# Tile 1's GLA output split around tile 0's first head, first experts from an 8 by 8 grid, gather buffers in another order

## The chip, the cores and the metric

One Trainium2 chip, one core of it. The metric is the device time of one execution of the whole program in microseconds (us), the median of several runs. TensorE (PE) multiplies, VectorE (DVE), ScalarE (ACT) and GpSimd (POOL) compute and issue DMAs, SyncE (SP) issues DMAs only, and 16 DMA engines carry the data.

## The reference

Two transformer-like blocks over 256 tokens of width 1024. The first block (recurrent unit, sparse attention, feed-forward) is not touched. The second has two layers, and each is a mixer with a layer norm and then a PEER layer with a layer norm. Layer 0's mixer is gated linear attention (GLA) beside attention over a memory:

```python
o = _gla(q, k, v, log_a)                       # 4 heads, chunks of 64 tokens
o = o * lax.rsqrt(jnp.mean(jnp.square(o), axis=-1, keepdims=True) + HEAD_NORM_EPS)
mix = silu(r) * (o * a_norm_g)
y = concatenate([mix, mo], axis=-1) @ w_out[l]
x = _layer_norm(DN_ALPHA * x + y, ln_mix_g[l], ln_mix_b[l])

q = (xt @ w_q).reshape(T, PEER_HEADS, 2, PEER_HALF)        # PEER: 8 heads
s = einsum('thpe,pne->thpn', q, sub_keys)                  # 2 x 128 key scores per head
top_s, top_i = lax.top_k(s, 16)
cand = top_s[:, :, 0, :, None] + top_s[:, :, 1, None, :]   # 16 x 16 candidates
best_s, best_j = lax.top_k(cand, 16)                       # 16 experts per head and token
expert = top_i[:,:,0][best_j // 16] * 128 + top_i[:,:,1][best_j % 16]
h = einsum('td,thkd->thk', xb, u[eb]); a = gelu(h) * softmax(best_s)
out = einsum('thk,thkd->td', a, v[eb])
```

So per layer every token takes 8 x 16 = 128 experts of 16384, each with a row u and a row v of 1024 floats.

## The kernel before, in words

Tokens lie on the 128 partitions, so the 256 tokens are two tiles, t = 0 and 1. The PEER work is a stream of 512 slots (2 layers x 2 tiles x 128 experts). For slot n GpSimd issues one indirect gather (`L2226`): for each of the 128 tokens of the tile one expert's u and v, 8 KB, into one of 8 buffers (`gbuf`, `GBUF`). VectorE takes the dot product of u with x (`L2510`), ScalarE applies gelu (`L2063`) and scales a diagonal matrix by it and the gate (`L2057`, `L2070`), TensorE multiplies the diagonal with v and adds in a PSUM bank (`add_slot`, `L1444`). That add frees the buffer, and GpSimd may issue gather n + 8.

Everything else of these layers is placed at slot numbers in tables (`pe_steps`, `act_steps`, `dve_steps`): an engine does a slot's steps and then the slot's own work. At slot 1 VectorE adds the mixer's output to tile 1's x (`second_sum`), at 3 it does its layer norm (`second_norm`), for which ScalarE takes the root in slot 2 (`second_root`), at 4 TensorE turns it, and at slots 6 and 9 it does tile 1's part of the first two heads (`tile_head`). From slot 8 on it does the next heads' queries (`head`) for both tiles, with weights from a ring of 8 slots (`weight_ring`), which SyncE fills in pairs, in order, as soon as TensorE has given both slots of a pair back.

The changed place is what stands ahead of slot 0, written out in order for each engine. TensorE: GLA output of tile 0, its mix turned, tile 0's output product (`out_rows`), tile 1's GLA output (`gla_out`, one call per pair of heads and half tile), tile 0's normed x turned (`turn_peer_half`), tile 0's first head (`head_tile`, queries, then `head_tile_keys`, scores), tile 1's mix turned (`turn_mix(1)`), tile 1's output product, tile 0's second head, and only then slot 0. VectorE: `mixed_tile(0)`, the sum and layer norm of tile 0, `mixed_tile(1)`, and then `first_head`, which routes the first head of tile 0: the best key pair (semaphore `first_expert`, gather 0), the next seven (`next_experts`, gathers 1 to 7), the other eight (`peer_experts`). ScalarE takes the squares of each GLA output (`gla_squares`) and copies banks to SBUF (`L1685`).

The gather buffers lie in the arena where the GLA's data lay: buffer place 0 over its queries, place 4 over the mixer's turned output (`mixT`), places 5 to 7 over its values, gates and states; the score rows `sc` overlap the end of the states. So gather 4 waits for tile 1's output (`MIX_BUF`). A wait on a PSUM job is a wait on one counter that TensorE raises per job (`psum_filled`), so jobs are numbered in TensorE's order (`plan`).

## Time and profile before

| what | value |
| --- | --- |
| time, median of 3 runs | 2069.57 us (2065.82 to 2070.25) |
| profiled execution, span | 2068.3 us; the page shows no time around it |
| busy: PE, DVE, ACT, POOL | 92%, 67%, 43%, 29% |
| DMA | 710.15 MB, mean 343 GB/s |
| of it gathers and other software DMAs (q0) | 550.15 MB |
| weights (q1) | 158.34 MB |
| add of slots, L1444 PE, x2048 | 975.7 us busy |
| dot of slots, L2510 DVE, x512 | 618.3 us busy, 448.3 idle before, of it 444.8 for the gather |

The page cuts the span into 40 slices and gives the busy share of each engine and of the DMA engines; windows do the same for any stretch. A timeline lists an engine's groups of instructions in order, with the idle time ahead of a group and what ended it. A 128x512 fp32 product leaves two records in the profile, so an add of a slot (two products) leaves four. Gather n is the n-th row of L2226.

### The profile page before, as it was taken

The page shows a single profiled execution, that of the slowest core. Times are in us where ns is not written, and L with a number is a line of the kernel's source. Part 1 is how long each engine was busy: PE and PEld are TensorE (multiplying, and loading weights), DVE is VectorE, ACT ScalarE, POOL GpSimd, SP SyncE. Part 2 cuts the span into 40 slices and gives each one's busy share as a digit, 9 for nine tenths or more (in the row PEclk, how much of TensorE's full clock was granted, in tenths as well). Part 3 has the DMA queues.
Part 4 walks back from the last instruction along what each step waited for, and adds up shares of the span by engine and source line. Part 5 has one row for each costly group of instructions (what it writes and reads, how often), then busy time and mean ns, then how long its engine had stood idle before and what let it go on. Part 6 is the DMA issues. An engine that isn't in the chain of part 4 may idle for free. (4 is left out here: it accounts for less than half of the span.)

```text
span 2068.3 us, 24678 instructions
## 1 busy us (share of the span) xinstructions
PE 1893.4 (92%) x8012; PEld 1183.8 (57%) x8012; DVE 1384.0 (67%) x2957; ACT 896.7 (43%) x2417; POOL 609.3 (29%) x563
## 2 busy tenths in 40 slices
PE   8999999999998999987999998889999989778776
PEld 7888678887964655533565534546675455332222
DVE  7788566666738776899534645667856466994444
ACT  5657454444634343344324623333455334343332
POOL 0002200000003434444433344333334433444442
PEclk9999999999999999999999999999999999999999
DMA  6633555554649999999999999999999999999997
GB/s 241 223 135 109 204 194 183 189 177 164 221 156 367 411 421 410 421 414 410 421 421 421 421 421 421 421 421 398 421 421 402 418 422 420 421 419 421 421 422 308
DMA packets 99373, 710.15 MB, mean 343 GB/s; under 512 B 11041, under 2 KB 11185, under 8 KB 14385
## 3 DMA queue, kind: packets, MB, share of 16 engines
q0 software_dynamic: 76928, 550.15, 64.6%
q1 hardware_dynamic: 22176, 158.34, 20.2%
q8 instruction: 64, 1.05, 0.2%
q14 instruction: 61, 0.49, 0.1%
q10 hardware_dynamic: 144, 0.11, 0.0%
HBM read 707.51 MB, written 1.05 MB: 343 GB/s over the span
## 5 line engine op out<-in xcount | busy, mean ns | idle before, releaser
L1444 PE MATMUL bank<-arena 128*128 128x512 f32 x2048 | 975.7, 614 | 147.9 <-ACT arena L2070 146.7
L2510 DVE SCALAR_TENSOR_TENSOR arena<-arena,x_tok 128x1024 f32<-128x1024 f32 x512 | 618.3, 1225 | 448.3 <-DMA arena<-peer_uv,arena 444.8
L2226 POOL DMA_INDIRECT arena<-peer_uv,arena x512 | 576.4, 1126 | 876.4 <-PE bank L1444 630.7
L1444 PEld LDWEIGHTS bank<-arena 128*128 128x128 f32 x2048 | 374.6, 194 | 629.7 <-issue 341.5
L2063 ACT ACTIVATE arena<-arena 128x1 f32<-128x1 f32 x512 | 103.1, 201 | 831.7 <-DVE arena L2510 830.8
L913 PEld LDWEIGHTS bank<-xT,weight_ring 128*128 128x128 f32 x1376 | 184.3, 194 | 39.1 <-issue 31.5
L2057 ACT ACTIVATE arena<-const_tile,arena 128x128 f32<-128x128 f32 x512 | 198.3, 387 | 0.0
L2070 ACT ACTIVATE arena<-arena 128x128 f32<-128x128 f32 x512 | 197.8, 386 | 0.8
L913 PE MATMUL bank<-xT,weight_ring 128*128 128x128 f32 (+1 forms) x1376 | 194.4, 295 | 0.8 <-DVE xT L2253 0.8
L913 PE MATMUL bank<-x_low_high,z_high 128*128 128x512 f32 (+1 forms) x480 | 135.5, 350 | 0.0
L1189 PE MATMUL bank<-x_split,w_split 128*128 128x512 f32 x704 | 129.2, 342 | 2.8 <-DVE x_split L2790 2.8
L1189 PEld LDWEIGHTS bank<-x_split,w_split 128*128 128x128 f32 x704 | 110.5, 191 | 20.2 <-issue 3.0
L2772 DVE TENSOR_TENSOR w_split<-weight_ring,w_split 128x1024 fp32r<-128x1024 f32 x66 | 80.8, 1225 | 36.8 <-ACT w_split L1898 36.0
L913 PE MATMUL bank<-x_low_high,ring_low 128*128 128x256 f32 x368 | 104.1, 283 | 0.0
L913 PEld LDWEIGHTS bank<-x_low_high,z_high 128*128 128x128 f32 x480 | 83.8, 191 | 14.9 <-issue 2.9
L1685 ACT ACTIVATE arena<-bank 128x512 f32<-128x512 f32 (+6 forms) x143 | 67.9, 499 | 53.0 <-PE bank L913 52.2
L859 POOL DMA_DIRECT2D row_ring<-rows_in x8 | 4.5, 571 | 288.1 <-DVEq L2326 200.8
L1898 ACT ACTIVATE w_split<-weight_ring 128x1024 fp32r<-128x1024 f32 x66 | 69.8, 1061 | 42.4 <-PE bank L1189 26.6
L913 PE MATMUL bank<-arena 128*64 128x128 f32 (+10 forms) x664 | 72.6, 305 | 1.7 <-DVE arena L2276 1.0
L913 PEld LDWEIGHTS bank<-x_low_high,ring_low 128*128 128x128 f32 x368 | 70.3, 191 | 0.0
L913 PEld LDWEIGHTS bank<-arena 64*128 64x128 f32 (+6 forms) x664 | 52.2, 161 | 26.6 <-issue 22.8
L913 PE MATMUL bank<-weight_ring,arena 128*128 128x512 f32 (+1 forms) x192 | 64.9, 528 | 0.2 <-ACT arena L1685 0.2
(321 smaller groups left out, 1991.9 us busy)
## 6 DMA issues: line engine op xcount, KB each, us to landing
weight_ring<-weights SPq DMA_DIRECT2D x149, 1024.0 KB, 4.9
arena<-peer_uv,arena POOLq DMA_INDIRECT x512, 13.7
row_ring<-rows_in POOLq DMA_DIRECT2D x8, 512.0 KB, 4.9
arena<-weights POOLq DMA_DIRECT2D x5, 512.0 KB, 7.9
kept_keys<-weights POOLq DMA_DIRECT2D x4, 512.0 KB, 10.0
const_tile<-consts POOLq DMA_DIRECT2D x1, 1657.0 KB, 8.3
x_tok<-x_in SPq DMA_DIRECT2D x2, 512.0 KB, 4.6
memT<-memT_in POOLq DMA_DIRECT2D x1, 1024.0 KB, 8.4
```

The lines of the kernel that those rows point to most:

```text
L859: e.dma_start(rows[:, n % NROW, :], rows_in[n:n + 1, :].to_broadcast([P, D]))\
L913: ins = pe.matmul(o, lhsT, rhs, start=start, stop=stop, is_transpose=turn or None)
L1189: ins = pe.matmul(o, lhsT, rhs, start=start, stop=stop)
L1444: ins = pe.matmul(b[:, :], diag[n % DIAGS], gbuf[n % GBUF][:, 1, h * 512:(h + 1) * 512], start=n % P == 0, stop=n % P == P - 1)
L1685: done(act.activation(o, i, f, **kw), "drained_by_act" if last else "act_step")
L1898: done(act.activation(w_split[n % SPLITS][:, 0, :], ring[:, slot % RING, :], ACT.Copy), "slot_high")
L2057: done(act.activation(gate_diag[n % 2], ident, ACT.Copy, scale=w[:, s:s + 1]), "gate_diag")
L2063: done(act.activation(hdot[:, s:s + 1], hdot[:, s:s + 1], ACT.Gelu), "peer_gelu")
L2070: done(act.activation(diag[n % DIAGS], gate_diag[n % 2], ACT.Copy, scale=hdot[:, s:s + 1]), "diag_ready")
L2226: pool.indirect_dma_start(gbuf[n % GBUF].rearrange("p a d -> p (a d)"), None, peer_uv, bass.IndirectOffsetOnAxis(ap=expert[t][:, s:s + 1]. ...
L2510: dve.scalar_tensor_tensor(u, u, 1.0, x[:, t, :], ALU.mult, ALU.mult, accum_out=hdot[:, s:s + 1])\
L2772: done(dve.tensor_tensor(w[:, 1, :], ring[:, slot % RING, :], w[:, 0, :], ALU.subtract), name)
```

## The change

Four edits. (1) TensorE: all but a part of tile 1's GLA output stands directly behind tile 0's output product; the second half tile of its last two heads stands around the scores of tile 0's first head. Of tile 1's output product, the three remaining pieces of its first two rows move behind that head, and the ring slots of these rows are given back there. (2) VectorE: the first expert and the next seven are found ahead of `mixed_tile(1)`, the latter from a grid of 8 by 8 candidates and not 16 by 16; the other eight come behind it, from a 16 by 16 grid into whose corner the 8 by 8 grid is copied with its best eight struck out. (3) ScalarE's order follows. (4) `GATHER_PLACES` gives gathers 0 to 7 the places 0, 1, 2, 3, 5, 6, 7, 4; gather 0 waits also for the last GLA product, gather 5 for tile 1's mix, gather 7 for tile 1's output.

TensorE, from tile 0's output product to slot 0, before (64x192: GLA output; x_tok: turn of x; xT,arena: head; weight_ring: output product; L1444: slots):

```order
L913 MATMUL bank<-weight_ring,arena 128x512 x16
L913 MATMUL bank<-arena 64x192 x4
L913 MATMUL bank<-const_tile,x_tok 128x128 x4
L913 MATMUL bank<-arena 64x192 x4
L913 MATMUL bank<-const_tile,x_tok 128x128 x4
L913 MATMUL bank<-arena 64x192 x8
L913 MATMUL bank<-xT,arena 128x128 x16
L913 MATMUL bank<-const_tile,arena 128x128 x8
L913 MATMUL bank<-weight_ring,arena 128x512 x12
L913 MATMUL bank<-xT,arena 128x128 x16
L913 MATMUL bank<-const_tile,arena 128x128 x2
L1444 MATMUL bank<-arena 128x512 x8
```

and the same place now:

```order
L914 MATMUL bank<-weight_ring,arena 128x512 x13
L914 MATMUL bank<-arena 64x192 x12
L914 MATMUL bank<-const_tile,x_tok 128x128 x8
L914 MATMUL bank<-xT,arena 128x128 x16
L914 MATMUL bank<-arena 64x192 x2
L914 MATMUL bank<-const_tile,arena 128x128 x2
L914 MATMUL bank<-arena 64x192 x2
L914 MATMUL bank<-weight_ring,arena 128x512 x3
L914 MATMUL bank<-const_tile,arena 128x128 x6
L914 MATMUL bank<-weight_ring,arena 128x512 x12
L914 MATMUL bank<-xT,arena 128x128 x16
L914 MATMUL bank<-const_tile,arena 128x128 x2
```

Three of the sixteen output products have moved from ahead of the first turn of x to ahead of the mix's turn (the row of x6), and of the sixteen GLA products all but four stand ahead of the turns. The x8 of const_tile,arena before is the mix's turn (6) and the keys (2), in this order.

VectorE, behind tile 0's layer norm, before (128x4 and 128x192: tile 1's mix; the rest: routing of the first head):

```order
L2941 RECIPROCAL arena<-arena 128x4
L2945 SCALAR_TENSOR_TENSOR arena<-bank,arena 128x192 x4
L2438 MAX arena<-arena 128x8 x2
L2441 MAX_INDEX arena<-arena 128x8 x2
L2443 CAST arena<-arena 128x2x8
L2444 TENSOR_SCALAR arena<-arena 128x1
L2445 TENSOR_TENSOR arena<-arena 128x1
L2448 MATCH_REPLACE arena<-arena 128x128 x2
```

and now, from the last three instructions of the next experts on:

```order
L2431 TENSOR_REDUCE arena<-arena 128x7
L2433 TENSOR_SCALAR arena<-arena 128x7
L2434 TENSOR_TENSOR arena<-arena 128x7
L2960 RECIPROCAL arena<-arena 128x4
L2964 SCALAR_TENSOR_TENSOR arena<-bank,arena 128x192 x4
L2471 MATCH_REPLACE arena<-arena 128x128 x2
L2474 MAX arena<-arena 128x8 x2
```

Tile 1's mix stood ahead of all routing, and stands now behind the experts 0 to 7. Between the first expert and the mix there are 16 instructions (lines 2456 to 2434).

The diff, cut:

```diff
@@ -40,7 +40,7 @@
 EXPERTS = PN * PN
 ALPHA = 4.0 ** 0.25
 GBUF = 8
-MIX_BUF = 4
+GATHER_PLACES = (0, 1, 2, 3, 5, 6, 7, 4)
 DIAGS = 5
 CARRY = 24
 LATER = 3
@@ -381,13 +381,13 @@
     plan("gla_o", 2, "dve", [0, 1])
     plan("gla_mixT_0", 2, "act", [6, 7])
     plan("out0_0", 2, "dve", [2, 3])
+    plan("gla_o", 1, "dve", [0], first=2)
     plan("xT_peer0_0", 1, "act", [6])
-    plan("gla_o", 1, "dve", [0], first=2)
     plan("xT_peer0_0", 1, "act", [7], first=1)
...
@@ -782,11 +782,12 @@
         mem_E = [area(24016 + 512 * b, 2, S) for b in range(3)]
         mem_PT = [area(25552 + 512 * b, 4, P) for b in range(2)]
 
-        gbuf = [area(2 * D * b, 2, D) for b in range(GBUF)]
         lo = 2 * D * GBUF
+        gbuf = [area(2 * D * b, 2, D) for b in GATHER_PLACES]
         sc = [area(lo + 2048 * t, 16, PN) for t in range(NT)]
         pq = [area(lo + 4096 + 512 * b, 2, S) for b in range(2)]
         rest = area(lo + 5120, 2 * TH * PN)
+        first_grid = area(lo + 5120 + 2 * PN, PK * PK // 4)
         onehot = area(lo + 5120, TH, PK, PK)
         top_v, top_i, top_f = (area(lo + 5632 + 64 * n, 2 * TH, PK) for n in range(3))
         best_v, best_j, pos_a, pos_b, sel_a, sel_b, pos_u = (area(lo + 5824 + 32 * n, TH, PK) for n in range(7))
@@ -1280,14 +1281,14 @@
                             mm(b[0:GDK, i * GDV:(i + 1) * GDV], kendT[o, n // 2, h, :],
                                gv[o, n // 2, h * GDV:(h + 1) * GDV], True, True, end=i == 1)
 
-                def gla_out(t, hp, pars):
+                def gla_out(t, hp, pars, heads=range(2)):
 
                     key = ("gla_o", 2 * t + hp)
                     b = begin(key) if pars[0] == 0 else bank(key)
                     for par in pars:
                         n = 2 * t + par
                         o = slice(par * CH, (par + 1) * CH)
-                        for i in range(2):
+                        for i in heads:
                             h = 2 * hp + i
                             vcol = slice(h * GDV, (h + 1) * GDV)
                             last = par == 1 and i == 1
@@ -1393,22 +1394,23 @@
             for h in range(2):
                 for k in range(NK - 2):
                     out_rows(0, k, [h])
-            out_rows(1, NK - 2, [1])
-            out_rows(1, NK - 1)
-            give_back()
-            gla_out(1, 0, [0])
+            gla_out(1, 0, range(2))
+            gla_out(1, 1, [0])
             pe.wait_ge(sem("x_half_ready"), 1)
             turn_peer_half(0, 0)
-            gla_out(1, 0, [1])
             pe.wait_ge(sem("x_ready"), 5)
             turn_peer_half(0, 1)
-            gla_out(1, 1, range(2))
             wait_drained(pe, ("xT_peer0_0", 1))
             pe.wait_ge(sem("head_loaded"), 64)
             head_tile(0, 0, 0)
             head_tile(0, 1, 0)
+            gla_out(1, 1, [1], [0])
+            head_tile_keys(0, 0)
+            gla_out(1, 1, [1], [1])
+            out_rows(1, NK - 2, [1])
+            out_rows(1, NK - 1)
+            give_back()
             turn_mix(1)
-            head_tile_keys(0, 0)
             wait_drained(pe, ("gla_mixT_1", 1))
             for k in range(NK - 2):
                 out_rows(1, k)
@@ -2077,13 +2079,13 @@
                 gla_squares(i)
             mix_turned(0)
             norm_root(0, 0)
+            gla_squares(2)
             turned_peer_half(0, 0)
-            gla_squares(2)
             turned_peer_half(0, 1)
+            head_tile(0, 0)
+            head_tile_keys(0, 0)
             gla_squares(3)
-            head_tile(0, 0)
             mix_turned(1)
-            head_tile_keys(0, 0)
             gate_exp(0, 0, 0, 1)
             head_tile(1, 0)
             head_tile_keys(1, 0)
@@ -2211,6 +2213,7 @@
             for n in range(SLOTS):
                 l, t, s = slot_of(n)
                 if n == 0:
+                    wait_filled(pool, ("gla_o", 3))
                     pool.wait_ge(sem("first_expert"), 1)
                 elif n == 1:
                     pool.wait_ge(sem("next_experts"), 1)
@@ -2218,7 +2221,9 @@
                     pool.wait_ge(sem("peer_experts"), ROUTE_NO[0, 0, 0])
                 elif (l, t, s) in ROUTE_NO:
                     pool.wait_ge(sem("peer_experts"), ROUTE_NO[l, t, s])
-                if n == MIX_BUF:
+                if n == GATHER_PLACES.index(6):
+                    pool.wait_ge(sem("mix_ready"), 2)
+                if n == GATHER_PLACES.index(4):
                     wait_filled(pool, ("out0_1", 1))
                 if n >= GBUF:
                     wait_freed(pool, n - GBUF)
@@ -2411,29 +2416,28 @@
...
-            def ranks_to_experts(l, t, h, first, last, name):
+            def ranks_to_experts(first, last, bits, name):
...
-            def first_head():
+            def first_expert():
+
+                half = PK // 2
                 wait_drained(dve, ("peer_s0_0_0", 0))
...
@@ -2444,6 +2448,25 @@
                 step(dve.tensor_scalar(sel_a[:, 0, 0:1], top_f[:, 0, 0:1], float(PN), 0.0, ALU.mult, ALU.add))
                 step(dve.tensor_tensor(expert[0][:, 0:1].bitcast(U32), sel_a[:, 0, 0:1], top_f[:, 1, 0:1], ALU.add),
                      "first_expert")
+
+            def next_experts():
+
+                half, lowest = PK // 2, -3.0e38
+                grid = rest[:, 0:half * half]
+                step(dve.tensor_tensor(grid.rearrange("p (a b) -> p a b", a=half),
+                                       top_v[:, 0, 0:half].unsqueeze(2).to_broadcast([P, half, half]),
+                                       top_v[:, 1, 0:half].unsqueeze(1).to_broadcast([P, half, half]), ALU.add))
+                best, at = best_v[:, 0, 0:half], best_j[:, 0, 0:half].bitcast(U32)
+                step(dve.max(best, grid))
+                step(dve.max_index(at, best, grid))
+                step(dve.match_replace(first_grid, best, grid, lowest))
+                ranks_to_experts(1, half, 3, "next_experts")
+
+            def other_experts():
+
+                half, lowest = PK // 2, -3.0e38
+                keys = sc[0][:, 0:2, :]
+                left = rest[:, 0:2 * PN].rearrange("p (a n) -> p a n", a=2)
                 for q in range(2):
                     done(dve.match_replace(left[:, q, :], top_v[:, q, 0:half], keys[:, q, :], lowest), "dve_step")
                 settle()
@@ -2455,20 +2478,16 @@
                 settle()
                 step(dve.tensor_copy(top_f[:, 0:2, half:PK], top_i[:, 0:2, half:PK].bitcast(U32)))
                 flat = keys.rearrange("p a n -> p (a n)")
-                step(dve.tensor_tensor(flat.rearrange("p (a b) -> p a b", a=PK),
-                                       top_v[:, 0, :].unsqueeze(2).to_broadcast([P, PK, PK]),
+                grid = flat.rearrange("p (a b) -> p a b", a=PK)
+                step(dve.tensor_tensor(grid, top_v[:, 0, :].unsqueeze(2).to_broadcast([P, PK, PK]),
                                        top_v[:, 1, :].unsqueeze(1).to_broadcast([P, PK, PK]), ALU.add))
+                step(dve.tensor_copy(grid[:, 0:half, 0:half], first_grid.rearrange("p (a b) -> p a b", a=half)))
                 best, at = best_v[:, 0, :], best_j[:, 0, :].bitcast(U32)
-                step(dve.max(best[:, 0:half], flat))
-                step(dve.max_index(at[:, 0:half], best[:, 0:half], flat))
-                ranks_to_experts(0, 0, 0, 1, half, "next_experts")
-                others = rest[:, 0:2 * PN]
-                step(dve.match_replace(others, best[:, 0:half], flat, lowest))
-                step(dve.max(best[:, half:PK], others))
-                step(dve.max_index(at[:, half:PK], best[:, half:PK], others))
+                step(dve.max(best[:, half:PK], flat))
+                step(dve.max_index(at[:, half:PK], best[:, half:PK], flat))
                 step(dve.tensor_tensor(gate_w[0][:, 0, :], best, best[:, 0:1].to_broadcast([P, PK]), ALU.subtract),
                      "peer_shifted")
-                ranks_to_experts(0, 0, 0, half, PK, "peer_experts")
+                ranks_to_experts(half, PK, 4, "peer_experts")
                 normalised_gates(0, 0, 0, 1)
 
             def experts(l, t, h, size):
@@ -2974,8 +2993,10 @@
             mixed_tile(0)
             first_sum()
             first_norm()
+            first_expert()
+            next_experts()
             mixed_tile(1)
-            first_head()
+            other_experts()
             for n in range(SLOTS + 2 * LATER + 1):
                 for name, what in DVE_STEPS.get(n, []):
                     if name == "second_sum":
```

## Rows read from the trace of the kernel before

**Rows 1.** The page's second part: DMA busy tenths in 40 equal slices.
```profile
DMA  6633555554649999999999999999999999999997
```

**Rows 2.** Windows around tile 1's mix: busy per engine, PEclk, DMA share, GB/s.
```profile
610.00:615.00 5.00, 5.00 (x24) 2.12 (x22) 0.00 (x0) 1.45 (x6) 0.00 (x0) 1.00 0.34 143
615.00:620.00 5.00, 5.00 (x42) 4.63 (x42) 1.57 (x5) 1.71 (x7) 0.00 (x0) 1.00 0.00 0
624.00:628.00 4.00, 4.00 (x11) 1.75 (x10) 3.65 (x15) 0.00 (x0) 1.00 (x1) 1.00 0.57 176
628.00:632.00 4.00, 4.00 (x16) 2.19 (x15) 3.55 (x15) 0.22 (x1) 1.23 (x2) 1.00 1.01 406
640.00:644.00 4.00, 3.87 (x6) 1.26 (x5) 2.10 (x3) 1.90 (x4) 0.48 (x1) 0.50 1.01 426
```

**Rows 3.** TensorE timeline: start, us, line, out<-in, count [idle before <- releaser].
```profile
606.85 1.94 PE L913 MATMUL bank<-arena 64*64 64x192 f32 x8
...
615.50 3.84 PE L913 MATMUL bank<-xT,arena 128*128 128x128 f32 x32
619.18 1.35 PE L913 MATMUL bank<-const_tile,arena 128*128 128x128 f32 x10
620.74 10.57 PE L913 MATMUL bank<-weight_ring,arena 128*128 128x512 f32 x24 [0.21 <-ACT arena L1685]
631.14 3.73 PE L913 MATMUL bank<-xT,arena 128*128 128x128 f32 x32
635.35 0.71 PE L913 MATMUL bank<-const_tile,arena 128*128 128x128 f32 x4 [0.47 <-ACT arena L1685]
...
638.92 6.56 PE L1444 MATMUL bank<-arena 128*128 128x512 f32 x8 [2.86 <-ACT arena L2070]
```

**Rows 4.** VectorE timeline, same columns, 617 to 648 us.
```profile
617.19 1.39 DVE L2945 SCALAR_TENSOR_TENSOR arena<-bank,arena 128x192 f32<-128x192 f32 x4
620.99 0.49 DVE L2438 MAX8 arena<-arena 128x8 f32<-128x128 f32 x2 [2.42 <-ACT arena L1685]
...
626.90 0.28 DVE L2423 TENSOR_TENSOR arena<-const_tile,arena 128x112 f32<-128x112 f32 x1
...
629.36 0.17 DVE L2429 TENSOR_TENSOR arena<-arena 128x7 uint32<-128x7 f32 x1
...
636.34 1.28 DVE L2519 SCALAR_TENSOR_TENSOR x_tok<-x_tok,bank 128x512 f32<-128x512 f32 x2
...
640.73 1.23 DVE L2510 SCALAR_TENSOR_TENSOR arena<-arena,x_tok 128x1024 f32<-128x1024 f32 x1 [1.56 <-DMA arena<-peer_uv,arena]
...
644.60 0.16 DVE L2340 RECIPROCAL arena<-arena 128x1 f32<-128x1 f32 x1 [0.24 <-ACT arena L1693]
...
647.77 1.23 DVE L2510 SCALAR_TENSOR_TENSOR arena<-arena,x_tok 128x1024 f32<-128x1024 f32 x1 [0.15 <-DVE x_tok L2343]
```

**Rows 5.** GpSimd timeline, same columns: gathers 0, 1 and 18.
```profile
623.99 1.01 POOL L2226 DMA_INDIRECT arena<-peer_uv,arena  x1 [32.53 <-issue]
630.47 0.98 POOL L2226 DMA_INDIRECT arena<-peer_uv,arena  x1 [5.46 <-DVE arena L2429]
...
677.58 0.94 POOL L2226 DMA_INDIRECT arena<-peer_uv,arena  x1 [3.46 <-PE bank L1444]
```

**Rows 6.** DMA issues, median us to landing: windows 623:625, 638:640, 677:679.
```profile
arena<-peer_uv,arena POOLq DMA_INDIRECT x1, 5.6
...
arena<-peer_uv,arena POOLq DMA_INDIRECT x2, 16.8
...
arena<-peer_uv,arena POOLq DMA_INDIRECT x1, 6.3
```

**Rows 7.** Windows, columns as in Rows 2, beside the first heads.
```profile
660.00:670.00 10.00, 10.00 (x41) 6.63 (x40) 8.16 (x24) 5.46 (x13) 1.92 (x2) 1.00 1.01 421
...
680.00:684.00 4.00, 4.00 (x20) 2.85 (x19) 2.11 (x12) 0.66 (x2) 1.27 (x3) 1.00 0.95 354
```

**Rows 8.** TensorE timeline: tile 1's first head at slot 6.
```profile
657.09 3.73 PE L913 MATMUL bank<-xT,arena 128*128 128x128 f32 x32
```

More of the change, by code:

```diff
@@ L2412, in best_pairs @@
                                        ALU.subtract), "peer_shifted")
-            def ranks_to_experts(l, t, h, first, last, name):
-                n = last - first
-                oh = onehot[:, 0, 0:n]
+            def ranks_to_experts(first, last, bits, name):
+                n, side = last - first, 1 << bits
+                oh = onehot[:, 0, 0:n, 0:side]
                 for q, (pos, sel) in enumerate(((pos_a, sel_a), (pos_b, sel_b))):
-                    op, val = (ALU.logical_shift_right, 4) if q == 0 else (ALU.bitwise_and, 15)
+                    op, val = (ALU.logical_shift_right, bits) if q == 0 else (ALU.bitwise_and, side - 1)
                     pos, sel, at = pos[:, 0, 0:n], sel[:, 0, 0:n], pos_u[:, 0, 0:n].bitcast(U32)
```

16 lines of the change are left out of this document (7 added, 9 removed).

## The prediction

> **What bounds the kernel now.** I read the page's slices of the DMA engines first [rows 1]. From the thirteenth slice (some 620 us) to the thirty-ninth they are nine tenths busy or more: the stream of 512 expert gathers and the weight loads fill them, and rows 7 give that stream's rate, 421 GB/s. Before it the load is light. So the kernel has two parts: a front whose length is set by the engines, and a stream whose length is set by bytes. The change works on the seam, so I went there. Windows [rows 2] show the seam: 0.34 busy in 610 to 615 (one pair of weight slots, 1.05 MB, is loaded there), nothing in 615 to 620, 0.57 in 624 to 628 with the lone first gather, then full. The timelines of TensorE, VectorE and GpSimd [rows 3 to 5] give the chain: scores of tile 0's first head at 620.99, first gather issued at 623.99, the next at 630.47.
>
> The next question is whether the stream is bound by bytes from its first microsecond on. It is not. A gather issued at about 639 lands 16.8 us later, one issued alone 5.6 us later, and gather 18, issued at 677.58, lands 6.3 us later [rows 5, 6]: the queue had nearly run dry, and in 680 to 684 the DMA share falls to 0.95 and the rate to 354 GB/s [rows 7]. Gather 18 waits for its buffer, and its releaser is the weighted add on TensorE (L1444). TensorE is busy for 10.00 of 10 us in 660 to 670 [rows 7], where it has the heads' queries to do between the adds. So between the start of the stream and slot 18 TensorE's chain eats the lead of the DMA queue, and at slot 18 it is TensorE's chain, not the first gather, that says when the stream goes on. Every microsecond by which that chain is later is a microsecond of the end; a gather that starts earlier buys nothing if the lead is used up anyway.
>
> **The change part by part, first gather.** The three output products (0.44 us a record [rows 3], two records each) leave the path: the GLA output follows at 606.85 - 3 x 0.88 = 604.2. It issues 24 records before the turns, at 1.94 / 8 = 0.24 each: 610.0. Eight turning products, at 1.35 / 10 each, give 611.1, and the copy of the second half about 0.9 more: head at 612.0 instead of 615.50 [rows 3]. After 3.68 of head come four GLA records (0.9), in which ScalarE copies the queries out, then the keys, 0.5: done at 617.1. Before, TensorE's row of turns and keys ends at 620.53 and VectorE starts at 620.99, so now 617.6, 3.4 us earlier, and the first gather is issued at about 620.6 instead of 623.99. Its new wait, for the last GLA product, ends at about 618 and hides behind that. GpSimd has nothing else queued there.
>
> **Second gather.** From gather 0 to gather 1 before: 630.47 - 623.99 = 6.5 us [rows 5]. Now 16 listed VectorE instructions lie between, the smallest like the 0.17 of L2429, the widest under the 0.28 of 112 elements [rows 4], with some 0.03 between them: 3.2 to 5.0 us, I take 3.8. Gather 1 is issued at 624.4, 6.1 us earlier. Gathers 2 to 4 follow freely; gather 5 waits for tile 1's mix (625.0, hidden), gather 7 for tile 1's output.
>
> **What the same reordering costs.** VectorE ran tile 1's mix at 617.19 for 1.39 us, with a reciprocal ahead, before the scores came [rows 4]: it was free there, since VectorE stood idle for 2.42 us behind it. Now it comes behind the next experts: 617.6 + 1.9 + 3.8 = 623.3, and 1.6 us for it gives 625.0. TensorE has by then done the last GLA records (to 618.0) and the three output products (to 620.7) and waits 4.4 us. Behind that wait are queued, in order, the turn of the mix, tile 1's output, the second head and the add of slot 0. The turn starts at 625.1 instead of 619.18, and from its start to the output it takes 1.56 as before [rows 3]: output at 626.7 instead of 620.74, **6.0 us later**. Output (10.4), head (3.7) and keys last as before, so the output is done at 637.2 and the add of slot 0 starts at 638.92 + 6.0 = 644.9.
>
> Not all of this reaches slot 18, for there was slack: before, VectorE's dot of slot 1 waited 1.56 us for its gather [rows 4]. It ended at 641.96 and the reciprocal of tile 1's layer norm came 2.64 later, at 644.60; between lie slot 1's work on ScalarE, a table load and the root. Now the gather is there long before, and ScalarE can do slot 1 only after slot 0, so the root follows the add of slot 0: 644.9 + 2.6 = 647.5, 2.9 us later than 644.60. The sum into tile 1 (636.34 before) starts at 637.2 and does not decide. From the reciprocal on the order is as it was: dot of slot 3 at 647.77 + 2.9, the head at slot 6 at 657.09 + 2.9 [rows 4, 8], and TensorE without a gap from there to slot 10, which frees gather 18's buffer.
>
> **The clock.** TensorE's gap of 2.86 us at 636 [rows 3] was followed by a granted clock of 0.50 in 640 to 644 [rows 2], that is 1.2 GHz and not 2.4, and the eight records behind it took 6.56 us where 8 x 0.44 = 3.5 is normal. So such a gap has cost 3.0 us. The new gap of 4.4 us stands ahead of the turn and the output; the old one stays. Its price is between 0 and 3.0; part of the slow time falls into the gap itself and into the wait for the mix's copy, and I take 1.2, of which half shows at slot 3 since VectorE and ScalarE have little slack there: 0.6. The Trainium skill (TensorE: Matmul & The Clock Gate, "The HAM clock gate") says that the half clock is the state of an idle array and that activity releases it; by that rule the new gap costs its full slow time, 1.2 us or more on the sum, and the trace agrees with the mechanism, with its 0.50.
>
> **What comes back.** Before, the stream already lost (421 - 354) x 4 / 421 = 0.6 us in 680 to 684 [rows 7] while gather 17 was still running; now the queue is dry ahead of 18 and the two no longer share. Between 0 and 1.1 us returns; I take 0.5.
>
> **The sum.** 2.9 + 0.6 - 0.5 = +3.0 us, bounds 2.9 - 1.1 = 1.8 and 2.9 + 3.0 = 5.9. The profiled span is 2068.3 us and nothing is shown around it: 2071.3. It lies 1.3 under the median of 2069.57, so the median should be **2072.6**. Reordering the buffers, the smaller grid and the 64-element copy cost some 0.3 us of VectorE ahead of slot 0, hidden behind tile 1's output (experts ready at about 632, output at 637.2).
>
> **Rivals.** (a) *Slower by more.* The chain from the late mix is worse than summed: both gaps give slow adds, gather 8 is issued only after slot 0's slow add (about 650 to 652), slots 3 to 6 are spread out, and the dry queue lasts longer. It decides from the point where slot 6's head starts later than about 661.5. At 6.0 us the whole delay of slot 0 reaches the end: 2068.3 + 6 = 2074.3, the median 2075.6. For it: rows 7 show no idle TensorE time to catch up with. Against it: the 1.56 us of slack in rows 4. (b) *Bytes bind.* If the stream's start counts and not slot 18, the lead of 3.4 us is kept. But the weight pair that lay in idle time at 610 to 612 is freed only by the first turn of the mix, now at 625, in full traffic: 1.05 MB / 421 GB/s = 2.5 us. Net -0.9, or up to -1.7 with the 0.8 us lost between gathers 0 and 1. Median 2068.3. For it: rows 1. Against it: the 6.3 us of gather 18 [rows 6]. The Trainium skill (DMA: Bandwidth & Descriptors, "Where 436 GB/s comes from") has a load from HBM bound at some 358 GB/s; by that the pair would cost 2.9 us and the net be -0.5, but the trace has 421 and decides. (c) *A real gain.* Gather 1's 6.1 us count, and the pair is absorbed: up to -5, median 2064.6. It needs a dry stream at its start and a full one at slot 18, and rows 2 show it full from 628 on.
>
> **How the numbers follow.** Forecast 50%, (a) 24%, (b) 20%, (c) 6%. A change under 0.2% (4.1 us) can't be told from none here. The forecast (1.8 to 5.9 with the medians' own scatter of some 2 us) is slower by over 0.2% in a quarter of its cases, (a) in five sixths, (b) hardly, (c) faster in most: faster 0.06, same 0.61, slower 0.33. The range leaves out (c) and the worst of (a): 2066.5 to 2077.0; the forecast's own is 2070 to 2075.5.
>
> **What would show it.** First gather issued near 620.6 and second near 624.4; the mix of tile 1 near 623.5; a TensorE gap of over 4 us near 621 to 625 with a clock of 0.5 behind it; tile 1's output from about 626.7; slot 0's add at 645 to 646; slot 6's head at 660 to 661.5; a DMA share under 1 before gather 18's data at about 681 to 684. The prediction is wrong if slot 6's head does not start later than 657, or if it does and the DMA engines are never idle before 690.

## The result: what the change did to the time

| | before | changed |
|---|---|---|
| median of 6 runs, us | 2069.74 (2065.82 to 2071.30) | 2074.82 (2073.99 to 2076.96) |
| span of the profiled execution, us | 2068.3 | 2072.8 |
| granted clock of TensorE, mean | 0.983 | 0.983 |

The ratio of the times is 1.0029, 95% interval 1.0019 to 1.0039: the changed kernel is slower, by 5.1 us by the medians and 6.0 by the ratio. The span of its profiled execution is 4.5 us longer, so the two profiles show the effect. Its own time is 2074.57 us, 1.8 over its span. One slow execution of the kernel before, of 10812.59 us, which fell among the later runs, is left out of all ratios below.

The page's DMA slices have the shape of [rows 1]: light up to the twelfth slice (three of the first twelve read a tenth lower), full from the thirteenth on:

```profile
DMA  6633555544539999999999999999999999999997
```

Everything ahead of the seam is in step. VectorE aggregates the statistics of tile 0's layer norm at 605.91 us before and at 605.95 now; I count from this point (**the anchor**) wherever kernels are compared below, since the work ahead of it ends some us earlier or later from run to run (at 602.7 to 611.0 in the runs below).

TensorE's timeline of the changed kernel, to be held against [rows 3, 8]:

```profile
604.32 5.68 PE L914 MATMUL bank<-arena 64*64 64x192 f32 x24
...
611.83 3.84 PE L914 MATMUL bank<-xT,arena 128*128 128x128 f32 x32 [0.80 <-ACT xT L1687]
...
616.53 0.71 PE L914 MATMUL bank<-const_tile,arena 128*128 128x128 f32 x4
...
618.11 2.84 PE L914 MATMUL bank<-weight_ring,arena 128*128 128x512 f32 x6
625.19 1.54 PE L914 MATMUL bank<-const_tile,arena 128*128 128x128 f32 x6 [4.24 <-DVEq L2968]
627.26 12.15 PE L914 MATMUL bank<-weight_ring,arena 128*128 128x512 f32 x24 [0.54 <-ACT arena L1687]
639.25 3.73 PE L914 MATMUL bank<-xT,arena 128*128 128x128 f32 x32
643.46 0.71 PE L914 MATMUL bank<-const_tile,arena 128*128 128x128 f32 x4 [0.47 <-ACT arena L1687]
647.03 7.11 PE L1446 MATMUL bank<-arena 128*128 128x512 f32 x12 [2.86 <-ACT arena L2072]
...
661.79 3.73 PE L914 MATMUL bank<-xT,arena 128*128 128x128 f32 x32
```

Tile 0's head starts at 611.83 instead of 615.50. Then comes the gap of 4.24 us, its releaser VectorE's mix, and behind it the turn at 625.19 instead of 619.18. From the turn's start to the next head it now takes 2.1 us more (14.06 us, not 11.96, though the keys' products no longer stand in between). Slot 0's add starts 8.1 us later, slot 6's head 4.70 us later.

VectorE [rows 4]. The 0.17 us row of L2434 is the last of the next experts, the row of L2964 tile 1's mix, now behind them; the reciprocal is that of tile 1's layer norm:

```profile
617.76 0.49 DVE L2442 MAX8 arena<-arena 128x8 f32<-128x128 f32 x2 [7.83 <-ACT arena L1687]
...
623.28 0.17 DVE L2434 TENSOR_TENSOR arena<-arena 128x7 uint32<-128x7 f32 x1
...
623.70 1.39 DVE L2964 SCALAR_TENSOR_TENSOR arena<-bank,arena 128x192 f32<-128x192 f32 x4
...
641.74 1.22 DVE L2529 SCALAR_TENSOR_TENSOR arena<-arena,x_tok 128x1024 f32<-128x1024 f32 x1
...
649.52 0.16 DVE L2345 RECIPROCAL arena<-arena 128x1 f32<-128x1 f32 x1 [5.40 <-ACT arena L1695]
```

The dot of slot 1 at 641.74 waits for no gather any more (1.56 us before), and VectorE then stands 5.40 us ahead of the reciprocal, which comes at 649.52 instead of 644.60.

GpSimd [rows 5], gathers 0, 1, 7, 8 and 18:

```profile
620.74 1.01 POOL L2231 DMA_INDIRECT arena<-peer_uv,arena  x1 [29.23 <-issue]
624.39 0.98 POOL L2231 DMA_INDIRECT arena<-peer_uv,arena  x1 [2.64 <-DVE arena L2434]
...
640.43 0.94 POOL L2231 DMA_INDIRECT arena<-peer_uv,arena  x1 [8.86 <-PE bank L914]
651.14 1.99 POOL L2231 DMA_INDIRECT arena<-peer_uv,arena  x1 [9.78 <-issue]
...
682.28 0.94 POOL L2231 DMA_INDIRECT arena<-peer_uv,arena  x1 [4.23 <-PE bank L1446]
```

Gathers 0 and 1 are issued 3.25 and 6.08 us earlier. Gather 8, which needs the buffer that slot 0's add frees, is 7.6 us later counted from the anchor, and gather 18 is 4.70 us later. Two things come before that. The lead is gone at gather 7, which waits for tile 1's output (place 4) and is issued 1.6 us later than before, behind the anchor, where gather 6 was still 6.9 us earlier. And gather 18 is not alone: from gather 11 to gather 52 every one is issued 4.4 to 4.8 us later, nearly all of them 4.65; TensorE's adds free their buffers. I go on naming gather 18, as the prediction does. The windows [rows 2, 7] show what the stream makes of that:

```profile
624.00:628.00 4.00, 2.27 (x7) 1.64 (x8) 3.66 (x18) 1.64 (x3) 2.85 (x3) 0.50 0.85 289
628.00:632.00 4.00, 4.00 (x8) 1.62 (x7) 3.59 (x14) 0.73 (x2) 2.81 (x3) 0.69 1.00 420
...
652.00:656.00 4.00, 3.56 (x10) 1.30 (x9) 3.81 (x13) 1.57 (x6) 3.15 (x3) 1.00 0.96 369
656.00:660.00 4.00, 3.19 (x15) 1.60 (x13) 3.86 (x13) 1.87 (x5) 0.95 (x2) 1.00 0.97 350
...
670.00:680.00 10.00, 10.00 (x41) 7.17 (x40) 8.03 (x18) 3.03 (x12) 3.48 (x3) 1.00 0.87 301
```

In 624 to 628 the DMA engines are at 0.85 where they were at 0.57: the stream does start earlier. What it gains is lost in hollows, at 652 to 660 (369 and 350 GB/s) and at 670 to 680 (301 GB/s at a share of 0.87, with TensorE busy for the whole 10 us). From 670 to 692 (344 GB/s in the last 12 us) the traffic that is missing against 421 GB/s is (120 x 10 + 77 x 12) / 421 = 5.0 us; before it was 1.3 us by the same sum (411 and 384 GB/s). The clock of 0.50 and 0.69 in the first two rows is the one behind the new gap.

### The profile page after: what moved, and what is told of

It is laid out like the page before. It is cut to its first block and busy times, and to the rows that moved or that the text cites. A ratio compares the mean times of both kernels' runs of the same rounds, so it can differ in the third digit from the quotient of the medians.

```text
span 2072.8 us, 24681 instructions
## 1 busy us (share of the span) xinstructions
PE 1892.0 (91%) x8012; PEld 1183.8 (57%) x8012; DVE 1383.4 (67%) x2959; ACT 896.3 (43%) x2417; POOL 611.7 (30%) x563
```

## The experiments

**Theory A**, that of the prediction: tile 1's mix is late, so TensorE's chain from the turn to slot 18 is late, and that chain sets when the stream goes on; early gathers buy nothing. **Theory B**, its rival: the bytes bind from the start of the stream, and a pair of weight slots that was loaded in idle time is now loaded in full traffic. (It is: the load of 1024 KB issued in 605 to 612 landed after 4.9 us before, and the one issued in 624 to 630 takes 10.1 us now.) All ratios are to the kernel before, timed on the same chip; a ratio need not equal the quotient of the two medians. Times in the last four columns are us behind the anchor.

| kernel | median, us | ratio (95%) | gather 0 | slot 0's add | gather 18 | end of span |
|---|---|---|---|---|---|---|
| before | 2069.74 | | 18.08 | 33.01 | 71.67 | 1462.39 |
| changed | 2074.82 | 1.0029 (1.0019 to 1.0039) | 14.79 | 41.08 | 76.33 | 1466.85 |
| changed, again | 2076.69 | 1.0045 (1.0032 to 1.0058) | 14.79 | 41.88 | 77.12 | 1468.98 |
| mix between | 2067.05 | 0.9992 (0.9982 to 1.0001) | 14.80 | 35.14 | 70.38 | 1460.64 |
| mix first | 2069.13 | 0.9996 (0.9987 to 1.0005) | 18.35 | 35.13 | 71.10 | 1462.05 |
| mix later still | 2081.76 | 1.0063 (1.0048 to 1.0078) | 14.79 | 49.04 | 84.28 | 1474.12 |
| pair early | 2078.32 | 1.0035 (1.0021 to 1.0050) | 17.36 | 45.03 | 80.28 | 1471.68 |
| grid only | 2068.33 | 0.9999 (0.9990 to 1.0008) | 18.08 | 33.01 | 70.45 | 1460.77 |
| clock kept up | 2073.81 | 1.0021 (1.0010 to 1.0031) | 14.79 | 39.05 | 74.30 | 1466.58 |
| light, changed | 2072.30 | 1.0011 (0.9999 to 1.0023) | 14.78 | 41.86 | 71.93 | 1464.71 |
| light, before | 2069.86 | 0.9998 (0.9988 to 1.0009) | 18.09 | 33.02 | 68.77 | 1462.66 |
| table early, before | 2069.42 | 1.0004 (0.9995 to 1.0012) | 18.09 | 33.89 | 71.37 | 1462.09 |
| mix between, table early | 2068.88 | 0.9994 (0.9984 to 1.0005) | 14.80 | 33.42 | 71.47 | 1462.12 |

The kernel before had medians of 2069.08 to 2069.74 in the four groups of runs.

### Tile 1's mix directly behind the first expert

```diff
             first_expert()
-            next_experts()
             mixed_tile(1)
+            next_experts()
             other_experts()
```

> The changed kernel with one move: VectorE does tile 1's mix between the first expert and the next seven. Theory A (the late mix delays TensorE's chain, and that chain at slot 18 sets the end): the mix ends at about 621.2 instead of 625.1, TensorE's gap of 4.2 us shrinks to some 0.4, its clock does not fall there, slot 0's add starts at about 641 instead of 647.0 and slot 6's head at about 656 to 657 instead of 661.8. The time comes back to that of the kernel before or 1 us below it: 2068.5 to 2070, 5 us under the changed kernel. Theory B (bytes bind; the weight pair that lost its idle slot is the cost): gather 1 is issued 1.7 us later than in the changed kernel and the pair 3.9 us earlier, still in traffic; under 1 us of change, about 2074.

TensorE's timeline, which starts 2.7 us earlier here (the anchor is at 603.26), and the window that was hollow, taken at the same place behind the anchor:

```profile
618.60 0.87 PE L914 MATMUL bank<-const_tile,arena 128*128 128x128 f32 x6 [0.34 <-DVEq L2968]
620.22 10.57 PE L914 MATMUL bank<-weight_ring,arena 128*128 128x512 f32 x24 [0.74 <-ACT arena L1687]
...
638.40 7.11 PE L1446 MATMUL bank<-arena 128*128 128x512 f32 x12 [2.86 <-ACT arena L2072]
...
653.16 3.73 PE L914 MATMUL bank<-xT,arena 128*128 128x128 f32 x32
```

```profile
667.00:677.00 10.00, 10.00 (x39) 6.40 (x38) 4.91 (x10) 4.62 (x17) 4.64 (x4) 1.00 1.00 395
```

The gap is down to 0.34 us, the turn and the output take their old 0.87 and 10.57 us, slot 6's head is 5.9 us earlier than in the changed kernel behind the anchor, the window has a DMA share of 1.00 and 395 GB/s, and the whole loss is gone (2067.05, under both forecasts). Gather 0 is where it was and gather 1 is 1.7 us later than in the changed kernel. One line of VectorE's order carries the loss; the earlier GLA output, the smaller grid and the buffers' order all stay in. The pair comes earlier too: its load is issued 15.8 us behind the anchor and lands after 7.0 us, for the most part beside gather 0 alone, where it was 19.9 and 10.1. That could give back B's 2.5 us at most, and 6.2 came back at the end of the span. Theory A.

### Tile 1's mix ahead of the first expert, as before

```diff
             first_norm()
+            mixed_tile(1)
             first_expert()
             next_experts()
-            mixed_tile(1)
```

> The changed kernel with VectorE's old order: tile 1's mix ahead of all routing. TensorE, ScalarE and the buffer places stay as changed. The mix must wait for the late GLA products: it ends at about 621.1, the first gather is issued at about 624.1 (as before the change) and the next at about 627.9, 3.4 us later than in the changed kernel. Theory A: slot 0's add at about 641, slot 6's head at 656 to 657, the time that of the kernel before, 2069 to 2070. Theory B: the stream starts 3.4 us later than in the changed kernel, with the weight pair still in traffic: 2076 to 2078.

Gather 0 is now at 18.35, 3.6 us later than in the changed kernel, and gather 1 at 22.01, 3.6 later too. The end is 4.8 us earlier all the same, and the median, 2069.13, is where A put it; B had 2076 to 2078. The pair is not still in traffic, as I had expected: its load is issued 15.8 us behind the anchor, ahead of gather 0, and lands after 4.7 us. With 2.5 us back for that and a start 3.6 us later, B still has the end 1 us later. A later start of the stream with an end that much earlier is what B can't have.

### The mix later still

```diff
                 ranks_to_experts(half, PK, 4, "peer_experts")
+                mixed_tile(1)
                 normalised_gates(0, 0, 0, 1)
...
             next_experts()
-            mixed_tile(1)
             other_experts()
```

> The changed kernel with the same wait made longer: tile 1's mix stands behind the routing of all 16 experts of the first head, only the gates' norm comes after it. Theory A: the mix ends 7.3 us later (about 632.3), TensorE's gap grows to about 11.5 us, slot 0 and slot 6's head come 7 us later, and so does the end: 2082. Theory B: the gathers are issued as before but for 5 and 6, and the bytes are the same: 2075 to 2076.

```profile
629.40 1.54 PE L914 MATMUL bank<-const_tile,arena 128*128 128x128 f32 x6 [11.63 <-DVEq L2969]
631.48 12.72 PE L914 MATMUL bank<-weight_ring,arena 128*128 128x512 f32 x24 [0.53 <-ACT arena L1687]
```

The mix is 7.4 us later than in the changed kernel, the gap 7.4 us longer, gather 18 is 8.0 us and the end 7.3 us later, with gathers 0 and 1 where they were. The medians differ by 6.9 us, where B had at most 1. Once the slack is used up, a microsecond of the mix is about one of the end.

### The pair of weight slots freed in idle time

```diff
+            out_rows(1, NK - 2, [1])
+            out_rows(1, NK - 1)
+            give_back()
             gla_out(1, 0, range(2))
...
             gla_out(1, 1, [1], [1])
-            out_rows(1, NK - 2, [1])
-            out_rows(1, NK - 1)
-            give_back()
             turn_mix(1)
```

> The changed kernel with the first three output products of tile 1 and the giving back of their ring slots ahead of the GLA output, as before the change. The weight pair moves in idle time again. Theory A: everything behind is later by the 2.6 us of these products (first gather at about 623.3, the mix ends at about 627.7, TensorE's gap stays, slot 6's head at about 664.4), the time about 2077. Theory B: 2.5 us of bytes leave the busy time and the stream starts 2.6 us later: 2075, no change.

```profile
630.24 1.54 PE L914 MATMUL bank<-const_tile,arena 128*128 128x128 f32 x6 [7.03 <-DVEq L2968]
```

This takes away B's cost: the pair is loaded by 614, in idle time, in 4.8 us. But it also makes the stream start 2.6 us later, so that B had forecast no change (2075) and A 2077. The three products and their pair are back ahead of the head, so head, scores, mix and turn are all 2.6 us later, and the gap grows by the work that was moved out of it. The output then takes 13.53 us and not 12.15, so that gather 18 is 4.0 us and the end 4.8 us later than in the changed kernel. That is more than A needs, but the profiled execution, 2081.91, was the slowest of five. The ratio, 1.0035, lies between the two of the changed kernel. By the times this experiment decides nothing; B fell with the three before it.

### The smaller grid alone, on the kernel before

The kernel before, with `first_expert()`, `next_experts()` and `other_experts()` of the changed kernel in the place of `first_head()`; the mix stays ahead.

> The kernel before with one part of the change: the next seven experts come from the 8 by 8 grid; the orders of all engines, the mix ahead of the routing and the buffer places are those of before. Gather 1 is issued at about 627.9 instead of 630.5. Theory A: slot 0's add stays at 638.9, the dot of slot 1 no longer waits 1.6 us for gather 1, the layer norm of tile 1 and slot 6's head come 1.5 us earlier, and the end 1.1 to 1.5 us earlier: 2068.4. Theory B: the stream starts 2.6 us earlier with the weight pair still in idle time, up to 2.6 us less: 2067.2.

VectorE, the dots of slots 1 and 2 and the reciprocal (the anchor is at 603.03):

```profile
635.81 1.23 DVE L2525 SCALAR_TENSOR_TENSOR arena<-arena,x_tok 128x1024 f32<-128x1024 f32 x1
...
638.42 1.23 DVE L2525 SCALAR_TENSOR_TENSOR arena<-arena,x_tok 128x1024 f32<-128x1024 f32 x1 [1.37 <-DMA arena<-peer_uv,arena]
...
639.69 0.16 DVE L2341 RECIPROCAL arena<-arena 128x1 f32<-128x1 f32 x1
```

Gather 1 is 2.9 us earlier and its dot waits no more; the next dot then waits 1.37 us for gather 2. Of the 2.9 us, 1.2 reach gather 18, and the times resolve no gain (0.9999), though the profile ends 1.6 us earlier. The change's own profit is therefore small even where nothing spoils it.

### Dummy products in the gap

```diff
             give_back()
+            for i in range(4):
+                pe.matmul(ps[2][:, :], ident, c("keysT"), start=True, stop=True)
             turn_mix(1)
```

> The changed kernel with four products of 128x512 (constants, result never read) that TensorE does while it waits for tile 1's mix. Theory A with the clock as a part of it: the wait of 4.2 us is mostly filled, the granted clock stays at 1.00 through the turn and tile 1's output, these take 2.1 us less (0.8 and 10.6 instead of 1.5 and 12.15), slot 6's head starts at about 659.7, and the time falls by 1.5 to 2.1 us to about 2073. If the clock costs nothing at the end, and theory B: no change, 2075.

TensorE, and the window of its turn and output:

```profile
621.05 3.60 PE L1414 MATMUL bank<-const_tile 128*128 128x512 f32 x8
...
625.47 0.87 PE L914 MATMUL bank<-const_tile,arena 128*128 128x128 f32 x6 [0.82 <-DVEq L2970]
627.09 10.57 PE L914 MATMUL bank<-weight_ring,arena 128*128 128x512 f32 x24 [0.74 <-ACT arena L1689]
...
660.03 3.73 PE L914 MATMUL bank<-xT,arena 128*128 128x128 f32 x32
```

```profile
625.00:629.00 4.00, 2.79 (x11) 1.60 (x12) 3.63 (x18) 2.16 (x3) 3.08 (x4) 1.00 0.84 289
```

The four products leave eight records. The turn starts at the same moment as in the changed kernel (625.47 with an anchor 0.27 later), so nothing but the clock differs, 1.00 where it was 0.50: 0.87 us against 1.54, 10.57 against 12.15. Slot 0's add, slot 6's head and gather 18 all come 2.0 us earlier. So in this pair of executions the clock's price is 2.25 us on the two rows and 2.0 on the chain (0.2 goes into the wait for the mix's copy, 0.54 us against 0.74). At the end the profile shows 0.3 us of it, and the ratios (1.0021 against 1.0029 and 1.0045) overlap. Issues of later gathers, us behind the anchor, say where it went:

| gather | 18 | 48 | 64 | 256 | 500 |
|---|---|---|---|---|---|
| before | 71.7 | 150.9 | 196.7 | 736.4 | 1407.9 |
| changed | 76.3 | 155.6 | 200.0 | 741.1 | 1412.4 |
| clock kept up | 74.3 | 153.5 | 200.1 | 739.9 | 1412.1 |
| mix between | 70.4 | 150.1 | 195.5 | 735.2 | 1406.2 |
| mix later still | 84.3 | 163.5 | 209.1 | 748.5 | 1419.8 |
| changed, again | 77.1 | 156.4 | 201.4 | 742.7 | 1414.6 |
| light, changed | 71.9 | 154.5 | 198.6 | 738.2 | 1410.3 |
| light, before | 68.8 | 150.2 | 197.3 | 736.8 | 1408.2 |

The 2.0 us stand at gather 48 and are gone at 64. The stretch from 48 to 64 took 44.1 to 47.1 us in the thirteen traces, so an execution loses or gains 1 to 2 us there whatever went before. The two executions of the changed kernel lie 0.8 us apart at gather 18 and 2.1 at the end. Whether the clock's 2 us reach the end is not settled.

### TensorE relieved

```diff
                 w = next_weights()
-                for k in range(NK):
+                for k in ((0, NK - 1) if h == 2 else range(NK)):
                     mm(b[:, q * S:(q + 1) * S], w[:, k * P:(k + 1) * P], xT[:, k, :], k == 0, k == NK - 1,
```

This edit was made to the changed kernel and to the kernel before. It leaves out six of the eight pieces of each query product of the third head.

> The changed kernel, with most of the queries of the third head left out: six of eight 128-row pieces of each of its two products (slots 8 and 10), so its routing is of another head; all gathers, dots and adds stay. TensorE has 5.4 us less to do ahead of slot 10's add, which frees gather 18's buffer. Theory A: gather 18 is issued up to 5.4 us earlier than at 682.3, the hollow in the DMA rate between 670 and 692 (5 us of traffic missing by the changed kernel's windows) fills, and the time falls by 3 to 5 us, to 2070 to 2072. Theory B: the same bytes, no change, 2075.

> The kernel before with the same queries of the third head left out. Its DMA rate misses only 1.1 us of traffic in 680 to 688. Theory A: about 1.1 us less, 2068.6, so that the two kernels with the light head differ by 1.5 to 3 us instead of 5. Theory B: no change, 2069.7, and the difference stays 5.

```profile
675.00:685.00 10.00, 10.00 (x31) 5.28 (x31) 8.78 (x21) 6.06 (x24) 6.34 (x6) 1.00 0.95 310
685.00:697.00 12.00, 12.00 (x44) 7.49 (x43) 8.61 (x30) 3.33 (x13) 4.88 (x5) 1.00 0.96 399
```

The rows are of the changed kernel so relieved (anchor at 610.99, 5 us later, so they are the stretches 670 to 680 and 680 to 692 of above). Gather 18 comes 4.4 us earlier than in the changed kernel, but the first stretch stays hollow (310 GB/s, 301 above) and only the second fills (399, 344 above): the missing traffic falls from 5.0 us to 3.3. Its median falls from 5.1 us over the kernel before to 2.4 over the relieved kernel before. That one gains nothing by the same edit, though its gather 18 is 2.9 us earlier; I had expected 1.1 us of it.

How the half came back is not shown. Of the 4.4 us at gather 18, 1.0 are left at gather 48, and the two relieved kernels stand 3.2 us apart at gather 18, 4.3 at gather 48 and 1.3 at gather 64: the difference shrinks in the stretch in which executions scatter by 1 to 2 us, not where TensorE was relieved. In both, gather 18 now lands 10.7 us after its issue and gathers 25 to 35 after 12 to 18 (8 to 13 in the kernels with the full head), so the queue is fuller there, and a gather that is issued earlier waits longer. By that reading TensorE's chain paces the stream in the kernels as they are, and relieved of 5.4 us of work no longer does. A holds for the delay and not for a gain of any size.

### The gelu's table loaded ahead of tile 1's head

```diff
             gate_exp(0, 0, 0, 1)
+            gate_diagonal(0)
+            done(act.activation(tmp_sq[:, GDV:GDV + 1], c("eps")[:, 0:1], ACT.Gelu), "act_step")
             head_tile(1, 0)
             head_tile_keys(1, 0)
-            gate_diagonal(0)
```

This takes the table load out of the 2.86 us gap of [rows 3], once on the kernel before and once together with the mix between.

> The kernel before with the same move on ScalarE alone (gate diagonal and gelu table ahead of the copies of the second head). Slot 0's add comes 1.6 us earlier, but the root of tile 1's layer norm waits for the dot of slot 1, which waits for gather 1 until 640.7 as before. Theory A: slot 6's head and gather 18 stay where they were and the time too, 2069.5, within 1 us. If slot 0's add alone set the end: 1.6 us less.

> The kernel of the first experiment (mix between first and next experts) with one more move on ScalarE: slot 0's gate diagonal and the load of the gelu table (by a gelu of one constant) stand ahead of the copies of the second head, no longer between the scores' copy and slot 0. TensorE's gap ahead of slot 0 (2.86 us) falls by 1.28 + 0.3 to about 1.2 us, its clock does not fall behind it, slot 0's add, the layer norm of tile 1 and slot 6's head come some 1.6 us earlier. Theory A: gather 18 is issued 1.6 us earlier; from there bytes bind, so of that at most the 1.4 us come back that the first experiment's windows still miss: 2065.5 to 2067.5, under both kernels. Theory B: nothing in the bytes is changed, as the first experiment.

On the kernel before, the move failed at what it was for: slot 0's add came 0.9 us later (33.89 against 33.01 behind the anchor), not 1.6 earlier. ScalarE's diagonal now waits 3.69 us for the gates from VectorE, ahead of the copies of the second head, and TensorE waits 2.56 us for these ahead of the keys (anchor at 604.71):

```profile
634.00 0.40 ACT L2057 ACTIVATE arena<-const_tile,arena 128x128 f32<-128x128 f32 x1 [3.69 <-DVE arena L2504]
...
636.24 1.22 PE L913 MATMUL bank<-const_tile,arena 128*128 128x128 f32 x4 [2.56 <-ACT arena L1685]
```

Gather 18 and the time stayed, but as slot 0's add was not made earlier, the question that was meant, whether that add alone sets the end, stays untested.

TensorE with both, anchor at 605.88:

```profile
639.30 3.70 PE L1446 MATMUL bank<-arena 128*128 128x512 f32 x8 [1.15 <-ACT arena L2072]
...
653.38 2.76 PE L1446 MATMUL bank<-arena 128*128 128x512 f32 x4 [1.95 <-ACT arena L2072]
655.95 4.65 PE L914 MATMUL bank<-xT,arena 128*128 128x128 f32 x32
```

The gap falls to 1.15 us and the eight records behind it take 3.70 us, not 6.56. Yet slot 6's head starts where it did with the mix between alone (50.07 against 49.90): a gap of 1.95 us appears at slot 5 and the head behind it takes 4.65 us instead of 3.73. Slot 0's add is 1.7 us earlier, as expected, but the saving turned into a later wait: gather 18 is 1.1 us later than with the mix between alone, not 1.6 earlier, and the median, 2068.88, misses the 2065.5 to 2067.5 that I had expected. No kernel of this study is measurably faster than the one before; the nearest is the mix between, at 0.9992 with an interval that reaches 1.0001.

### The changed kernel once more

The changed kernel, with no edit, beside the last two.

> The changed kernel itself, beside the two others on one chip, to have its ratio from the same run of rounds: 1.0029 of the kernel before, within 0.001.

It gave 1.0045 (1.0032 to 1.0058) beside the first 1.0029 (1.0019 to 1.0039), more than the 0.001 off that I had allowed. It is slower both times; what the two intervals share, 1.0032 to 1.0039, is 6.6 to 8.1 us, and their ends are 3.9 and 12 us. The loss is certain and its size is not. TensorE (anchor at 604.72) and the window behind slot 0's gap:

```profile
623.97 1.41 PE L914 MATMUL bank<-const_tile,arena 128*128 128x128 f32 x6 [4.26 <-DVEq L2968]
625.91 13.07 PE L914 MATMUL bank<-weight_ring,arena 128*128 128x512 f32 x24 [0.54 <-ACT arena L1687]
...
646.60 3.70 PE L1446 MATMUL bank<-arena 128*128 128x512 f32 x8 [2.86 <-ACT arena L2072]
```

```profile
647.00:651.00 4.00, 3.30 (x8) 1.14 (x6) 1.84 (x3) 3.86 (x7) 1.61 (x1) 1.00 1.02 424
```

The same gap of 4.26 us here makes the turn and the output 3.04 us longer, not 2.25. And the old gap of 2.86 us, behind which the kernel before had a clock of 0.50 and 6.56 us for eight records, has a clock of 1.00 behind it and 3.70 us. What a gap's slow clock takes is not one number. Nor does it always reach the chain: in seven traces (the changed kernel twice, mix between, mix later still, pair early, clock kept up, light changed) slot 6's head starts 14.76 or 14.77 us behind slot 0's add, with the slow clock behind the old gap or without it.

## Why the prediction held, and which term was too small

The time of 2074.82 us lies in the range (2066.5 to 2077.0), 2.2 over the forecast of 2072.6. The mechanism was right. The size was low by a half or more: +3.0 us forecast, 4.5 between the two profiles, 5.1 between the medians, 6.0 and 9.3 by the two ratios. With it I gave "slower by over 0.2%" too little, 0.33.

- **First and second gather.** Forecast 620.6 and 624.4, measured 620.74 and 624.39. Each was a sum of row durations on VectorE and TensorE, and such sums held to 0.1 us.
- **The late mix and the gap.** Mix done 625.0 forecast, 625.09 measured; gap 4.4 and 4.24; turn 625.1 and 625.19.
- **The clock: the mis-sized term.** I took 1.2 us for it, counted half, 0.6, and had argued that part of the slow time would fall into the gap and the wait for the mix's copy. Only 0.2 does: the turn and the output take 0.67 and 1.58 us more, 2.25 together, of which the dummy products gave 2.0 back as far as gather 18. In the repeat they take 3.04 more. The half for slack at slot 3 was wrong too: the 2.1 us by which slot 0's add was later than forecast (8.1 and not 6.0) were 2.0 at the reciprocal. My own bounds, 0 to 3.0, held it as it reached the chain. The old gap of 2.86 us had shown 3.0, and going by it would have come closer, but partly by luck: behind the same gap the repeat shows nothing, and in the changed order what was slow there never reached slot 6's head. What I had wrong is the place. The new gap stands ahead of the output product, and behind it TensorE works on through the second head with waits of 0.54 and 0.47 us only, so that its own rows are the chain and the slow time has little slack to fall into.
- **The slack.** 2.9 of the 6.0 us were to remain at the reciprocal, 2.6 us behind slot 0's add. Measured 2.49 behind it, and 4.92 us late, that is the 2.9 and 2.0 of clock. Slot 0's add itself came at 647.03, outside my 645 to 646, by the same 2.0.
- **On to slot 18.** "From the reciprocal on the order is as it was" held: +4.70 at slot 6's head and +4.70 at gather 18. That slot 18 is the place where the chain takes over did not: the delay has its 4.7 us from gather 11 on and keeps them to gather 52.
- **What comes back.** 0.5 forecast, 0.2 measured. In all 2.9 + 2.0 - 0.2 - 0.2 = 4.5 us, the difference of the spans (the first 0.2 from the reciprocal to slot 3's dot, the second behind gather 18). That this closes is a matter of these two executions: the delay is 3.2 us at gather 64 and 4.7 at 256, and the profile of the repeat stands 5.5 us behind at gather 18 and 6.6 at the end. The 0.5 is neither confirmed nor refuted.
- **Rival (a)** was to decide from 661.5 at slot 6's head; 661.79 is just past it. Its mark, gather 8 at 650 to 652, came true with 651.14, but not its price: of slot 0's 8.1 us 4.7 reached the end, since the 1.56 us wait and what lay behind it did absorb the rest. The case lies between the forecast and (a).
- **Rival (b)** fell with the mix put first, between and later still. Granted the pair's 2.5 us wherever its load had moved out of the traffic, it has the end 1 us later, at most 2.5 earlier and unchanged, and the profiles showed 4.8 earlier, 6.2 earlier and 7.3 later. No run excludes the pair from a part of the loss by itself, but the delay of gathers 11 to 52 is that of slot 6's head, 4.65 us, and leaves it no share there. Rival (c) fell with the loss and the hollows at 652 to 680.
- The Trainium skill's clock page (TensorE: Matmul & The Clock Gate, "The HAM clock gate"), by which an idle array is at half clock until activity releases it, spoke for the full slow time, 1.2 us or more. The trace agrees, with 0.50 in 624 to 628 and 2.25 us, and I gave it too little weight for this gap. Behind the old gap the two levels were both seen, 0.50 before and 1.00 in the repeat, and in the changed order neither moved slot 6's head against slot 0's add.

## What to carry to other kernels

Where an engine at ten tenths follows the start of a DMA stream, look for an issue at which the queue runs low (here gather 18, landing 6.3 us after its issue instead of 16.8) and count back from there: what stands on that engine's chain is worth its time, an earlier start of the stream little (2.9 us at gather 1 gave 1.2 at gather 18 and no gain that the times resolve). When work is moved ahead in an in-order engine, ask first what it overtakes; 1.4 us of mix that TensorE waits for, put behind 5.7 us of work whose earlier end bought nothing, cost 4.5 us. Charge a new gap on TensorE with the slow clock behind it in full where TensorE's own rows are the chain there, and not where the chain waits for other engines; here that was 2.3 to 3.6 us, and one profile doesn't give the number.

## What the runs showed of the hardware

- Behind the new gap on TensorE windows of 4 us show a granted clock of 0.50 to 0.69, and the turn and the output, 11.44 us together at 1.00 (0.87 and 10.57), took longer: 2.25, 3.04 and 3.03 us behind 4.24 to 4.26 us of gap (changed kernel, its repeat, light), 3.63 behind 7.03 us and 2.82 behind 11.63 us. So the price does not follow the length of the gap; equal gaps differ by 0.8 us. Gaps of 0.34 and 0.82 us left the rows as they were. Behind 1.95 us the head took 4.65 us and not 3.73.
- Behind 2.86 us of gap ahead of slot 0 the clock was 0.50 in the kernel before and 1.00 in the repeat of the changed kernel, eight records 6.56 and 3.70 us.
- Four products on constants, eight records and 3.60 us of them in the gap, kept the clock at 1.00: the row behind them, 0.82 us later, ran at its full speed.
- A gather's lead of 6.1 us was gone by gather 7 and a delay of 4.7 us from gather 11 on, with the DMA engines idle for parts of 652 to 680, although they had been at 0.85 to 1.00 in 624 to 632.
